# A new order for the first microseconds of a two-layer encoder trunk: norm weights turned first, first low parts between the input's copies, S5 angles behind the first scaling

## The reference

```python
def rmsnorm(x, g):
    return x * rsqrt(mean(x * x, axis=-1) + EPS) * g
def swiglu(x, w1, w3, w2):
    return (silu(x @ w1) * (x @ w3)) @ w2
for i in range(2):
    h = h + 0.5 * swiglu(rmsnorm(h, ffn1_norm[i]), ffn1_w1[i], ffn1_w3[i], ffn1_w2[i])
    h = h + mixer_i(rmsnorm(h, mix_norm[i]))          # S5, then attention
    h = h + 0.5 * swiglu(rmsnorm(h, ffn2_norm[i]), ffn2_w1[i], ffn2_w3[i], ffn2_w2[i])
    h = h + (p[i] @ ple_proj[i]) * sigmoid(rmsnorm(h, ple_norm[i]) @ ple_gate[i])
return rmsnorm(h, final_norm)

# S5 constants, from parameters alone:
dt = exp(log_dt); mag = exp(lam_re * dt)
abar_re, abar_im = mag * cos(lam_im * dt), mag * sin(lam_im * dt)
```

## Time and profile before

| what | us |
|---|---|
| median of 3 runs | 1148.19 |
| lowest and highest | 1147.57, 1150.16 |
| the profiled execution | 1145.03 |
| its span, first to last instruction | 1143.3 |
| TensorE busy | 1093.3 (96%) |
| its weight loads busy | 1000.7 (88%) |
| VectorE busy | 796.6 (70%) |
| ScalarE busy | 617.7 (54%) |
| GpSimd busy | 297.7 (26%) |
| mean granted TensorE clock, share of full | 0.983 |

### The profile page before, as it was taken

One profiled execution on the slowest core, in us unless ns is written; L12 is line 12 of the kernel. 1 busy time (PEld: TensorE's weight loads), 2 busy tenths in 40 slices (PEclk: granted clock), 3 DMA queues, 4 the chain that ended last, 5 costly groups with the idle time before them and its releaser, 6 DMA issues.

```text
span 1143.3 us, 18397 instructions
## 1 busy us (share of the span) xinstructions
PE 1093.3 (96%) x7350; PEld 1000.7 (88%) x7350; DVE 796.6 (70%) x927; ACT 617.7 (54%) x876; POOL 297.7 (26%) x294
## 2 busy tenths in 40 slices
PE   6899999989698999999999999999999999999997
PEld 6899999879698888888898888887988888888886
DVE  6788876788586777666686776665454676776665
ACT  6644444353757656554565565454556665555543
POOL 7799998951131100000210000011011110000021
PEclk9999999998799999999999999999999999999998
DMA  8565554331125565665555656555423356656552
GB/s 213 155 186 175 182 173 122 106 127 57 37 93 172 156 204 182 199 187 191 175 172 169 204 181 196 186 186 185 145 93 96 118 176 190 191 180 202 191 164 87
DMA packets 179707, 183.06 MB, mean 160 GB/s; under 512 B 16168, under 2 KB 173488, under 8 KB 179632
## 3 DMA queue, kind: packets, MB, share of 16 engines
q1 hardware_dynamic: 179488, 181.99, 51.5%
q10 hardware_dynamic: 144, 0.04, 0.0%
HBM read 180.95 MB, written 1.05 MB: 159 GB/s over the span
## 4 chain that ended last, share of the span: by engine, by line
PE 65%; DVE 8%; ACT 4%; issue 2%; POOL 2%; POOLq 0%; DVEq 0%; ACTq 0%
PE acc L1760 31%; PE acc L1762 16%; PE bank L1478 2%; DVE w_lo L987 2%; PE bank L1479 2%; PE bank L1480 2%; PE acc L1478 2%; PE acc L1480 2%; PE acc L1479 2%; ACT square_sum L876 1%; POOL square_sum L468 1%; DVE op_both L1000 1%; PE acc L1700 1%; PE acc L1686 1%; ACT u_steps L864 1%
## 5 line engine op out<-in xcount | busy, mean ns | idle before, releaser
L987 DVE TENSOR_TENSOR w_lo<-raw,w_hi 128x1024 fp32r<-128x1024 f32 x346 | 452.5, 1318 | 210.7 <-ACT w_hi L654 209.3
L654 ACT ACTIVATE w_hi<-raw 128x1024 fp32r<-128x1024 f32 x346 | 356.5, 1040 | 249.5 <-PE acc L1762 87.8
L1760 PE MATMUL acc<-op_both,w_hi 128*128 128x512 f32 x1056 | 368.6, 394 | 0.7 <-DVE op_both L1000 0.6
L1762 PE MATMUL acc<-op_both,w_lo 128*128 128x256 f32 x1056 | 294.9, 279 | 0.0
L1760 PEld LDWEIGHTS acc<-op_both,w_hi 128*128 128x128 f32 x1056 | 197.8, 187 | 46.0 <-DVE op_both L1000 1.3
L1762 PEld LDWEIGHTS acc<-op_both,w_lo 128*128 128x128 f32 x1056 | 199.2, 189 | 0.0
L1760 PE MATMUL acc<-g_all,w_hi 128*128 128x512 f32 x528 | 183.2, 392 | 0.0
L1478 PE MATMUL bank<-op_both,w_hi 128*128 128x256 f32 x576 | 170.6, 296 | 8.9 <-DVE op_both L1000 5.4
L1479 PE MATMUL bank<-op_both,w_lo 128*128 128x256 f32 x576 | 165.8, 288 | 0.0
L1480 PE MATMUL bank<-op_both,w_hi 128*128 128x256 f32 x576 | 165.8, 288 | 0.0
L464 POOL TENSOR_TENSOR square_sum<-squares 128x512 f32<-128x512 f32 x9 | 13.6, 1516 | 528.3 <-issue 527.7
(11 more groups left out here) (309 smaller groups left out, 1735.7 us busy)
## 6 DMA issues: line engine op xcount, KB each, us to landing
raw<-in_ffn_w_dram SPq DMA_DIRECT2D x258, 512.0 KB, 4.1
raw<-in_sb_w_qkv_dram SPq DMA_DIRECT2D x24, 512.0 KB, 3.5
raw<-in_s_w_glu_dram SPq DMA_DIRECT2D x16, 512.0 KB, 3.6
raw<-in_ple_gate_dram SPq DMA_DIRECT2D x16, 512.0 KB, 3.5
raw<-in_s_w_in_dram SPq DMA_DIRECT2D x8, 512.0 KB, 3.3
raw<-in_sb_w_o_dram SPq DMA_DIRECT2D x8, 512.0 KB, 3.4
raw<-in_ffn_w_dram SPq DMA_DIRECT2D x12, 256.0 KB, 3.2
raw<-in_ple_proj_dram SPq DMA_DIRECT2D x4, 512.0 KB, 3.7
```

The costliest lines, as they stand in the source:

```text
L654: act.activation(w_hi[:, slot, 0:width], raw[:, slot, 0:width], ACT.Copy).then_inc(hi_done, 1)
L987: dve.tensor_tensor(w_lo[:, slot, 0:width], raw[:, slot, 0:width], w_hi[:, slot, 0:width].bitcast(F32), ALU.subtract).then_inc(lo_done, 1)
L1760: pe.matmul(pairs[h][:, m].rearrange("p i t -> p (i t)"), wh, x.rearrange("p i t -> p (i t)"), start=first, stop=False, skip_group_check=True)
L1762: return pe.matmul(pairs[h][:, m, 0, :], wl, x[:, 0, :], start=False, stop=last, skip_group_check=True)
```

## The change

Five edits, all in the opening and the first group of the first feed-forward.

1. TensorE turns the norm weights ahead of the input, and so waits for their DMAs first.
2. VectorE copies two pairs of the input, splits chunk 0, takes the first two low parts, copies the third pair, takes the next two low parts, copies the fourth, and splits chunk 1.
3. VectorE computes the S5 angles behind the scaling of group 0's second result, and no longer between the diagonal and the split of chunk 5.
4. ScalarE takes SiLU of group 0 behind the split of chunk 5, ahead of `zero_state(1)` and `s5_phasors`. `first_state` stays last.
5. GpSimd clears `within[0]` while it waits for the mean, when TensorE has turned the C parameters. At the old place only a one-column tile `mark` is cleared, to signal.

```diff
@@ gpsimd
                     pool.memset(w_state_out[:, 0, NQ // 2:], 0.0).then_inc(state_zeroed, 1)
+                    pool.wait_ge(c_turned, 2)
+                    link(pool.memset(within[0][:, :, :], 0.0))
                 pool.wait_ge(mean_ready, v + 1)
...
                     if j == TAU:
-                        pool.memset(within[0][:, :, :], 0.0).then_inc(weights_ready, 1)
+                        pool.memset(mark[:, :], 0.0).then_inc(weights_ready, 1)
@@ scalar
                 split(n0 + 5)
+                do_silu(0)
                 if nxt.kind == "s5":
                     zero_state(1)
                     s5_phasors()
-                do_silu(0)
-                if nxt.kind == "s5":
                     first_state()
@@ vector
                     dve.tensor_tensor(b_n[:, :, :], bank[1][:, :, :], r_bc, ALU.mult).then_inc(b_taken, 1)
+                    if nxt.kind == "s5" and isinstance(g, int) and g == 0:
+                        s5_angles()
                     dve.wait_ge(silu_done, base + g + 1)
...
                 stat_diag(v)
-                if nxt.kind == "s5":
-                    s5_angles()
                 split(n0 + 5)
...
-            for b in range(NB):
+            def x_in(b):
                 dve.wait_ge(x_turned, b + 1)
                 dve.tensor_copy(xT[:, 2 * b:2 * b + 2, :], acc[b][:, :, :]).then_inc(x_new, 1)
+            x_in(0)
+            x_in(1)
             split(0)
             dve.wait_ge(gain_ready, 1)
             op_low(0, 0, 0)
+            x_in(2)
             op_low(0, 0, 1)
+            x_in(3)
             split(1)
@@ tensor
             pe.wait_ge(consts_ready, 5)
+            pe.wait_ge(gains_landed, 16 * 5)
+            R = 9 * KD
+            pe.transpose(misc[:, 0:R], gain_rows[0:R, :], ident[0:R, 0:R]).then_inc(gain_turned, 1)
             pe.wait_ge(rows_landed, 16 * TB)
             for k in range(KD):
...
-            pe.wait_ge(gains_landed, 16 * 5)
-            R = 9 * KD
-            pe.transpose(misc[:, 0:R], gain_rows[0:R, :], ident[0:R, 0:R]).then_inc(gain_turned, 1)
```

More of the change, by code:

```diff
@@ L164, in hybrid_trunk @@
         dt_rows = sb("dt_rows", [NQ, 2])
+        mark = sb("mark", [P, 1])
         g_all = sb("g_all", [P, 2 * NG, 2, T], F32R, at=mixer)
```

## The result

The changed kernel takes **1157.58 us** (median of 7 runs, 1154.84 to 1159.16), the kernel before, on the same chip, 1149.19 (7 runs, 1145.38 to 1152.55): ratio **1.0065, 95% interval 1.0043 to 1.0086**. So it is slower, by 4 to 8 us in the medians, where 3.9 were forecast. A ratio is an estimate of its own over the runs, and not the quotient of the two medians (1.0073 here). The profiled execution took 1157.58 us (span 1155.8, mean clock 0.983).

What follows compares the result with a forecast made beforehand. TensorE was taken to bound the kernel. Chunk 6 2.1 us later plus 1.8 us lost to the clock gave +3.9 us, a median of 1152.1 us from 1148.19; the 8-in-10 range was 1148.0 to 1154.5.

Steps and rivals of the forecast that it cites:

- chunk 5's rounding to SiLU: With the angles moved on VectorE, `a_n` would be ready at 30.9 us, not 32.42, after chunk 5's landing at 27.6.
- Part 1: Opening, norm weights first and copies apart: chunk 2's split, and so chunk 5's landing, 0.5 us later, bounds 0 and 2.3.
- Gains late: Rival in the opening: norm weights usable at 9.5 us or later, slip 1.5 to 2.3, total +4.9 to +5.7; chance 0.08.
- Part 3: ScalarE's SiLU ahead of clearing and phasors: 8.63 us behind 30.9 with a third table load, chunk 6 2.1 us later.
- The clock: Behind TensorE's new pause ahead of chunk 6, slow products would lose 1.8 us, bounds 0.5 and 2.85.
- GpSimd: Its chain ahead of the first S5 blocks would end at 159.5 us, before TensorE came near 164, costing nothing.
- The rival that ended faster: Chunk 6's low half there by 36.9 us, so TensorE runs through: −3.1 us, 1145.1; chance 0.08.
- the clock pays nothing more: Rival: chunk 6 starts at full speed after the pause, +2.1 us at most, 1150.3 or 1149; chance 0.15.
- the table that serves Exp: Rival on ScalarE: SiLU's table serves Exp, no third load, chunk 6 at 40.7, total +2.4 us, 1150.6; chance 0.17.
- a switch of twice its row: Rival on ScalarE: the third table load costs 1.4 us more, total +5.3 us, 1153.5; chance 0.02.

Runs made afterwards that it cites:

- first profile: Profile of the changed kernel from its first comparison with the kernel before: median 1157.58 us beside 1149.19, ratio 1.0065.
- second profile: Profile of the changed kernel when measured once more, unaltered, against the kernel before: median 1155.11 us beside 1150.93, ratio 1.0045.
- the copies apart alone: The kernel before with only the third and fourth copy of the input moved between the first low parts: median 1148.93 us, ratio 0.9994.
- the old order on ScalarE: The changed kernel with SiLU of group 0 again behind the phasors and the angles again ahead of chunk 5's split: median 1150.66 us, ratio 1.0009.
- ScalarE's part alone: The kernel before with SiLU ahead of the second clearing and phasors, and the angles behind the scaling: median 1154.57 us, ratio 1.0039.

## Why the prediction was wrong in its size

The direction, the place and the mechanism were right: the wait for `a_n` went to 1.10 us in the first profile (1.47 in the second) where 1.1 was forecast, TensorE then stood for chunk 6's low half behind ScalarE's list, with products at half clock behind it. What failed are two terms of the sum: the slip of chunk 5 was taken too small, and one table load was put at nothing. The forecast was 1152.1, the range to 1154.5, and the median is 1157.58. Of these 5.5 us, 1.0 is the kernel before, whose median was 1148.19 in the three runs shown and 1149.19 in the comparison. The sum by its own terms, with the two profiles of the changed kernel:

| term | predicted | first profile | second profile |
|---|---|---|---|
| slip of chunk 5's landing | 0.5 | 2.54 | 1.40 |
| chunk 5's rounding to SiLU | 3.3 | 3.41 | 3.42 |
| SiLU to the end of the first state | 8.63 | 8.63 | 8.62 |
| load at the loop | 0 | 1.28 | 1.28 |
| chunk 6 against 39.89 | +2.1 | +5.46 | +4.32 |
| lost to the clock behind it | 1.8 | 2.3 | 1.6 |
| lag at the first S5 block | +3.9 | +7.78 | +5.94 |

**Part 1, "I take 0.5 us for the split of chunk 2", failed: it was 1.4 to 2.5 at chunk 5's landing.** I had let the drawn-out low parts and the copies apart give back what the opening lost. With the norm weights there at 8.02 us, earlier than my 8.5, the slip is already 1.40. In the first profile the second pair of low parts takes 1.69 us where 0.8 was counted, and the split of chunk 1 takes 2.13 and not 1.2 (in the kernel before it had taken 1.58, which I did not count either). This is work drawn out beside GpSimd's sums, which now fall on an earlier place of VectorE's list. It is not the copies within the list that do it: with the copies apart alone the same pair took 0.87, since GpSimd's first sum came behind it, at 12.74. The first row is of that kernel; the second is of the changed one, whose pair starts at 14.72, within the sum:

```profile
11.85 0.87 DVE L1000 SCALAR_TENSOR_TENSOR op_both<-xT,gain,op_both 128x256 fp32r<-128x256 f32 x2
14.43 1.30 POOL L465 TENSOR_TENSOR square_sum<-squares 128x512 f32<-128x512 f32 x1 [2.03 <-ACT squares L673]
```

The last four low parts take 4.82 in place of 5.85, which is all that is given back. My upper bound, 2.3, was passed in the first profile: chunk 2's split came at 23.72, 2.60 late. "Gains late" had 0.08 of the chance; of its price, 1.5 to 2.3 for the slip, every profile has had nearly as much or more.

**Part 3 left out a load.** From SiLU to the end of the first state it was right to 0.01 us, with the third load. The next step, from the end of the first state straight to "rounding and low half of chunk 6", was wrong by 1.28: I had seen that the loop is entered with the sines' table and put the price into the rounds at SiLU, where it is hidden, but not at the entry, where nothing hides it.

**The clock** was right within its bounds. **GpSimd** was right in that nothing waits for it: the chain's end moved by 4.5 us, from 156.56 to 161.03, and TensorE's coming by more; but I had 159.5, for the phasors ended at 39.46 and not at 37.2.

**The range** took each bound by itself. The slip at its upper bound and the clock at its own, together, make 2.1 + 1.8 + 2.85 = +6.75, or 1155 by the forecast's base, outside of a range that ended at 1154.5. By my own chances it held 0.92 and not 8 in 10, as only the faster case lay outside.

**The rival that ended faster** is refuted: `w_lo` at 45 and not at 36.9. That the clock pays nothing more is refuted in both profiles, and so is the table that serves Exp. Against a switch of twice its row stand the rows: SiLU to the end of the first state took what single loads give, with two loads in it.

What remains is between the lag at 160 us and the medians. The first profile has +7.78 there and +8.4 in the medians, the second +5.94 and +4.2. That the second comparison's 4.2 is close to the forecast 3.9 is luck: in its trace the same two terms lie above the forecast's, and the lag is +5.94. The lag goes through the S5 stage with a shift of a microsecond or two either way. A fall of the clock at 354.2, which the kernel before does not have, cost some 2.7 us in the first profile (lag 6.02 at 345 of the kernel before, 8.71 at 354), as the fall at 351.1 did with the old order on ScalarE (3.06 and 5.66). What brings these falls is not shown.

## What to carry to other kernels

When a wait is shortened, look at which list it lies in: with ScalarE's part alone chunk 4 came 1.6 us earlier (30.97 in place of 32.55), but a list of 8.6 us and a load of ScalarE's now stood behind the same event, and chunk 6 came 3.3 us later. What a loop needs at its entry belongs to that list: ask with which table it is entered. And a small DMA that had landed in time when it was used second must be taken at its worst when it is used first.

## What the runs showed of the hardware

*A table load in front of a copy.* With the sines' table loaded at the entry of the loop, a load of 1.28 us stands before the rounding of chunk 6 (41.68), and two stand in each round (51.83, 57.56). With SiLU's table at the entry, or with ScalarE's first group written out, the load before the rounding is not there. That the state of the table has to be the same at the top of every round is my reading of it.

*Two spacings of the same products.* In the three feed-forward stages behind the first, the products of 512 and 256 columns come in pairs, a pair every 0.347 us or every 0.353. Mostly a stage has one of the two nearly from start to end, and which one changes from profile to profile. The kernel before has 0.347 in all three in its one profile; its near copy with only the copies apart has 0.353 in two of them. A group of the lines view, 430 to 500 us, before and after (68.7 us for 198 pairs, 70.4 for 199):

```profile
L1760 PE MATMUL acc<-op_both,w_hi 128*128 128x512 f32 x198 | 68.7, 394 | 0.0
```

```profile
L1766 PE MATMUL acc<-op_both,w_hi 128*128 128x512 f32 x199 | 70.4, 399 | 0.0
```

The slower one costs 1.8 to 2.5 us in a stage. Three such stages make nearly the spread of a kernel's own runs (7.2 us for the kernel before). The first profile of the changed kernel has two slow stages and that of the kernel before none, and they make 4 of its 12.6 us at the end. The cause stays open. Single runs can't be compared closer than this here; the start of one and the same early product can.
